# The opening of a hybrid decoder layer: rows normalised tile by tile, small transposes in other banks, the gate product on VectorE, the sample convolution between taps

## The reference, cut to what matters

```python
h = rmsnorm(x, norm_mix_g)
p = einsum('btd,dk->btk', h, w_in)          # 6 blocks of 1024 columns
u_a, v_a, c_val, c_gate, g_a, g_b = split(p)
glu = c_val * sigmoid(c_gate)
padded = concatenate([conv_buf, glu], axis=1)   # prompt: zeros; sample: 30 cached rows
conv = depthwise_conv(padded, conv_w) + conv_b  # 31 taps per channel
y_b = silu(layernorm(conv)) @ w_branch_b + b_branch_b
y_a = (u_a * chunk_spatial_mix(layernorm(gelu(v_a)))) @ w_branch_a
x = x + (sigmoid(g_a) * y_a + sigmoid(g_b) * y_b) @ w_out
x = x + moe(rmsnorm(x, norm_ffn_g))             # top 4 of 32 experts
```

## Time and profile before

| | us |
|---|---|
| median of 3 runs (1359.11 to 1364.49) | 1363.99 |
| the profiled execution, its own time | 1364.04 |
| span of that execution | 1362.3 |
| PE busy | 1196.0 (88%) |
| DVE busy | 584.2 (43%) |
| POOL busy | 494.5 (36%) |
| ACT busy | 255.3 (19%) |
| bytes read from HBM | 447.00 MB, 330 GB/s over the span |

### The profile page before, as it was taken

How to read it: one execution, slowest core, us unless ns; L and a number is a source line. 1 busy time by engine, 2 the same in 40 slices (tenths; PEclk the granted TensorE clock), 3 DMA queues, 4 the chain that set the end, 5 groups by cost and what they waited for, 6 DMA issues and landing times.

```text
span 1362.3 us, 30127 instructions
## 1 busy us (share of the span) xinstructions
PE 1196.0 (88%) x11131; PEld 585.9 (43%) x11132; DVE 584.2 (43%) x1229; ACT 255.3 (19%) x497; POOL 494.5 (36%) x813
## 2 busy tenths in 40 slices
PE   5899999999999997797699779869799798699996
PEld 3677777775543343232233223323234233233333
DVE  0699971211353443433244424424244344244444
ACT  3001122200122221221122112111122121122222
POOL 0183120000141344455444544544445445444330
PEclk9898999999799999998899889989899899899998
DMA  8963333345489599999999999999999999999981
GB/s 255 317 196 108 111 119 124 99 153 220 174 358 382 197 397 418 418 418 417 419 417 416 416 419 418 418 418 418 416 416 417 417 418 414 418 418 409 398 345 59
DMA packets 110953, 448.96 MB, mean 330 GB/s; under 512 B 8526, under 2 KB 42894, under 8 KB 78107
## 3 DMA queue, kind: packets, MB, share of 16 engines
q1 hardware_dynamic: 110190, 446.57, 83.0%
q10 hardware_dynamic: 685, 1.17, 0.3%
q0 software_dynamic: 48, 0.85, 0.2%
HBM read 447.00 MB, written 2.42 MB: 330 GB/s over the span
## 4 chain that ended last, share of the span: by engine, by line
PE 60%; DMA 11%; POOL 8%; issue 8%; DVE 7%; SPq 5%; ACT 0%; DVEq 0%; POOLq 0%
PE banks L1290 21%; PE banks L1093 12%; PE banks L1300 12%; DMA ring<-in_w_down 10%; POOL ring L508 6%; DVE R L762 4%; PE banks L1021 3%; SPq L383 3%; PE banks L1075 3%; PE banks L1054 2%; PE banks L1205 2%; POOL big L477 1%; PE banks L1061 1%; POOL prod L499 1%; PE banks L1084 1%
## 5 line engine op out<-in xcount | busy, mean ns | idle before, releaser
L1290 PE MATMUL banks<-ring,hT 128*32 128x512 f32 x3328 | 441.5, 625 | 99.1 <-POOL ring L508 84.2
L508 POOL COPY ring<-big 128x512 f32<-128x512 f32 x248 | 142.2, 621 | 567.9 <-SPq L389 567.9
L508 POOL COPY ring<-R 128x512 f32<-128x512 f32 x496 | 287.1, 623 | 133.4 <-DMA R<-in_w_up 131.2
L309 DVE TENSOR_TENSOR xt<-xt,banks 128x1024 f32<-128x1024 f32 x106 | 128.8, 1215 | 432.6 <-PE banks L1075 432.6
L1300 PE MATMUL banks<-ring,hT 128*32 128x256 f32 x3328 | 229.8, 396 | 11.5 <-DMA ring<-in_w_down 10.0
L1093 PE MATMUL banks<-hT,ring 128*128 128x288 f32 x768 | 195.6, 417 | 7.9 <-ACT stage L535 6.0
L1290 PEld LDWEIGHTS banks<-ring,hT 128*32 128x32 f32 x3328 | 98.7, 113 | 236.2 <-POOL ring L508 106.5
L1300 PEld LDWEIGHTS banks<-ring,hT 128*32 128x32 f32 x3328 | 110.5, 115 | 196.9 <-issue 129.4
L1093 PEld LDWEIGHTS banks<-hT,ring 128*128 128x128 f32 x768 | 149.3, 196 | 50.6 <-ACT stage L535 6.4
L654 ACT COPY WT<-banks 128x256 f32<-128x256 f32 x52 | 19.4, 372 | 537.9 <-PE banks L1300 537.9
L762 DVE SCALAR_TENSOR_TENSOR R<-big,convw,R 128x256 f32<-128x256 f32 x240 | 99.7, 490 | 0.0
(11 more groups left out here) (225 smaller groups left out, 770.3 us busy)
## 6 DMA issues: line engine op xcount, KB each, us to landing
ring<-in_w_down SPq DMA_DIRECT2D x128, 1024.0 KB, 11.7
R<-in_w_up SPq DMA_DIRECT2D x124, 1024.0 KB, 18.2
ring<-in_w_up SPq DMA_DIRECT2D x70, 1024.0 KB, 9.4
big<-in_w_up SPq DMA_DIRECT2D x62, 1024.0 KB, 14.1
ring<-in_w_in SPq DMA_DIRECT2D x24, 1024.0 KB, 10.0
ring<-in_w_branch_b SPq DMA_DIRECT2D x4, 1024.0 KB, 4.9
ring<-in_w_branch_a SPq DMA_DIRECT2D x4, 1024.0 KB, 4.9
ring<-in_w_out SPq DMA_DIRECT2D x4, 1024.0 KB, 4.9
```

Source lines behind the costliest of these rows:

```text
L309: nc.vector.tensor_tensor(dst, dst, rows, ALU.add).then_inc(y_added, 1)
L508: ins = nc.gpsimd.tensor_copy(ring[:, k, h * 512:(h + 1) * 512], parked[k][:, h * 512:(h + 1) * 512])
L1290: ins = mm(UP[g * BLK:(g + 1) * BLK, :], xT[:, k, :], ring[:, k, g * 512:(g + 1) * 512], start=k == 0, stop=k == UP_SLOTS - 1)
```

## The change

- The eight vector parameters are loaded from ACT's queue instead of SP's.
- ACT loads the root's table first, and squares, roots, scales and turns go tile by tile: DVE scales row tile tt as soon as its own root is there, and PE turns all eight pieces of it. PE runs 16 small matmuls of 128x32 ahead of that. The gain and the other vectors are turned between the second and third row tile. ACT scales the even tiles of `hT` on the way out, DVE the odd ones, and PE starts on each tile as it comes.
- After j = 0 the history is turned into banks 4 to 7 as before, but conv_w goes to bank 2, b_up to bank 3, and the spatial weights to banks 6 and 7; each step of j waits for its own banks.
- The copy of the value (ACT) goes away. DVE multiplies it straight out of PSUM with the sigmoid in `tmpc` (`gate`), tiles 0 and 1 ahead of the convolution, 2 and 3 after pair 0, 4 to 7 between taps of pair 1. PE waits for these products before it uses a bank again, and for all eight only before it turns v.
- DVE's eight sample tiles come between taps of pairs 2 and 3 instead of behind them.

```diff
@@ SP
-            for v, name in enumerate(vec_names):
-                load(vecrows[v * KC:(v + 1) * KC, :], a[name][0].rearrange("(c p) -> c p", p=P), vec_in)
@@ POOL
-            pool.wait_ge(evac_early, 5)
-            for c in range(KC):
-                pool.wait_ge(gate_sig, c + 1)
-                nc.gpsimd.tensor_tensor(cprompt[:, c, HIST:HIST + SEQ], tmpv[:, c % 2, 0:SEQ],
...
             pool.wait_ge(glu_ready, KC)
             nc.gpsimd.tensor_copy(glu_tail[:].rearrange("p c (b t) -> p c b t", b=DB),
                                   csample[:, :, :, HIST:SEG]).then_inc(tail_packed, 1)
 
+            pool.wait_ge(small_copied, 3)
@@ ACT
+            for v, name in enumerate(vec_names):
+                act.dma_start(vecrows[v * KC:(v + 1) * KC, :], a[name][0].rearrange("(c p) -> c p", p=P)
+                              ).then_inc(vec_in, 16)
             act.wait_ge(pads_zero, 1)
+            act.wait_ge(const_ready, 4)
+            load_root_table()
             for tt in range(NT):
...
-            act.wait_ge(const_ready, 4)
-            act.wait_ge(squared, NT)
-            root(ss[:, 4:4 + NT], ss[:, 0:NT], 1.0 / D)
+                act.wait_ge(squared, tt + 1)
+                root(ss[:, 4 + tt:5 + tt], ss[:, tt:tt + 1], 1.0 / D)
 
             act.wait_ge(evac_early, 1)
-            for c in range(KC):
+            for c in range(0, KC, 2):
                 act.wait_ge(x_transposed, c + 1)
...
-                nc.scalar.activation(tmpc[:, c % 2, :], bank[4 * (c // 2 % 2) + 2 + c % 2][:, 0:T], ACT.Sigmoid)
-                nc.scalar.copy(tmpv[:, c % 2, :], bank[4 * (c // 2 % 2) + c % 2][:, 0:T]).then_inc(gate_sig, 1)
+                nc.scalar.activation(tmpc[:, c % 2, :], bank[4 * (c // 2 % 2) + 2 + c % 2][:, 0:T], ACT.Sigmoid
+                                     ).then_inc(gate_sig, 1)
@@ DVE
+            for c in range(1, KC, 2):
+                dve.wait_ge(x_transposed, c + 1)
+                V.tensor_scalar(hT[:, c, :], bank[c][:, 0:T], col(NORM_MIX, c), None, ALU.mult).then_inc(hT_odd, 1)
...
+            def gate(c):
+
+                dve.wait_ge(gate_sig, c + 1)
+                val = bank[4 * (c // 2 % 2) + c % 2]
+                V.tensor_tensor(cprompt[:, c, HIST:HIST + SEQ], val[:, 0:SEQ], tmpc[:, c % 2, 0:SEQ], ALU.mult)
+                V.tensor_tensor(csample[:, c, :, HIST:SEG], val[:, SEQ:T].rearrange("p (b t) -> p b t", b=DB),
+                                tmpc[:, c % 2, SEQ:T].rearrange("p (b t) -> p b t", b=DB), ALU.mult
+                                ).then_inc(glu_ready, 1)
...
+            between = {(0, 30): (gate, (2, 3)), (1, 11): (gate, (4, 5)), (1, 26): (gate, (6, 7)),
+                       (2, 10): (convolve_sample, (0,)), (2, 20): (convolve_sample, (1,)),
+                       (2, 30): (convolve_sample, (2,)), (3, 6): (convolve_sample, (3,)),
+                       (3, 12): (convolve_sample, (4,)), (3, 18): (convolve_sample, (5,)),
+                       (3, 24): (convolve_sample, (6,)), (3, 30): (convolve_sample, (7,))}
@@ PE
+            for _ in range(16):
+                mm(bank[7][:, 320:320 + NE], ones[:], below[:, 0:NE], start=True, stop=True)
...
-            pe.wait_ge(hT_ready, KC)
             for j in range(KC // 2):
+                if j == 1:
+                    pe.wait_ge(history_copied, KC)
                 if j >= 2:
                     pe.wait_ge(gate_sig, 2 * (j - 1))
+                    pe.wait_ge(glu_ready, 2 * (j - 1))
+                if j == 2:
+                    pe.wait_ge(small_copied, 2)
                 for part in range(2):
+                    if j == 1 and part == 1:
+                        pe.wait_ge(small_copied, 3)
...
-            pe.wait_ge(gate_sig, KC)
+            pe.wait_ge(gate_sig, KC - 2)
+            pe.wait_ge(glu_ready, KC - 2)
@@ turn_v
+            if c == 0:
+                pe.wait_ge(gate_sig, KC)
+                pe.wait_ge(glu_ready, KC)
```

More of the change, by code:

```diff
@@ L703, in _ @@
                 r = ROWS[tt]
+                dve.wait_ge(rooted, tt + 1)
+                link(V.reciprocal(ss[:, 4 + tt:5 + tt], ss[:, 4 + tt:5 + tt]))
                 V.tensor_scalar(stage[0:r, tt, :], xs_rows if tt == 2 else xt[:, tt, :], ss[0:r, 4 + tt:5 + tt], None,
                                 ALU.mult).then_inc(xs_ready, 1)
[L707 to L711 removed]
@@ new lines, in _ @@
+            for c in (4, 5, 6, 7, 0, 1, 2, 3):
+                V.tensor_copy(csample[:, c, :, 0:HIST],
+                              bank[4 + c // 2][:, (c % 2) * DB * HIST:(c % 2 + 1) * DB * HIST]
+                              .rearrange("p (b h) -> p b h", b=DB)).then_inc(history_copied, 1)
+            dve.wait_ge(small_turned, 1)
+            V.tensor_copy(convw[:], bank[2][:, 0:KC * W].rearrange("p (c k) -> p c k", c=KC)
+                          ).then_inc(small_copied, 1)
+            dve.wait_ge(small_turned, 2)
@@ L749, in take_x, with convolve @@
                                 ).then_inc(xT_ready, 1)
-            def convolve(pair):
-                for k in range(W):
+            def gate(c):
[5 more added lines that the diff above has]
+                                ).then_inc(glu_ready, 1)
+            def convolve(pair, taps):
+                for k in taps:
                     for c in pair:
@@ L765, in convolve, with convolve_sample @@
                         link.count[0] += 1
-            def convolve_sample(tiles):
-                for c in tiles:
-                    dve.wait_ge(prod_ready, DS * (c + 1))
-                    tail = conv[:, c, SEQ:T]
-                    V.tensor_reduce(tail, prod[:].rearrange("p b t k -> p (b t) k"), AX.X, ALU.add
-                                    ).then_inc(prod_used, 1)
-                    dve.wait_ge(prod_used, c + 1)
-                    V.tensor_scalar(tail, tail, col(CONV_B, c), None, ALU.add).then_inc(conv_done, 1)
+            def convolve_sample(c):
+                dve.wait_ge(prod_ready, DS * (c + 1))
+                tail = conv[:, c, SEQ:T]
+                V.tensor_reduce(tail, prod[:].rearrange("p b t k -> p (b t) k"), AX.X, ALU.add
+                                ).then_inc(prod_used, 1)
+                dve.wait_ge(prod_used, c + 1)
+                V.tensor_scalar(tail, tail, col(CONV_B, c), None, ALU.add).then_inc(conv_done, 1)
+            between = {(0, 30): (gate, (2, 3)), (1, 11): (gate, (4, 5)), (1, 26): (gate, (6, 7)),
[3 more added lines that the diff above has]
+                       (3, 24): (convolve_sample, (6,)), (3, 30): (convolve_sample, (7,))}
             dve.wait_ge(history_zero, 1)
+            gate(0)
+            gate(1)
             for pair in range(KC // 2):
                 dve.wait_ge(glu_ready, 2 * pair + 2)
-                convolve((2 * pair, 2 * pair + 1))
-                if pair == 2:
-                    convolve_sample(range(0, 3))
-            convolve_sample(range(3, KC))
+                for k in range(W):
+                    convolve((2 * pair, 2 * pair + 1), (k,))
+                    if (pair, k) in between:
+                        what, tiles = between[pair, k]
+                        for c in tiles:
+                            what(c)
             dve.wait_ge(v_rows, 2 * KC)
```

79 lines of the change are left out of this document (35 added, 44 removed).

## The result

| us | before | after |
|---|---|---|
| median of six runs each | 1359.61 (1359.11 to 1364.49) | 1349.75 (1346.70 to 1353.98) |
| the profiled execution, its own time | 1364.04 | 1346.70 |
| its span | 1362.3 | 1344.8 |
| start of the mean over channels | 185.25 | 168.76 |
| start of w_out | 317.85 | 303.38 |

The medians differ by 9.9 us. The ratio of the times is 0.9916 (0.99 to 0.9932), which is 11.4 us. Six runs of the kernel before put its median at 1359.6. Four of them lie within 0.6 us of each other, two at about 1364, and the profiled execution, on which the prediction stood, was as long as those two. The profiled execution of after, in turn, is the shortest of its six.

The account below looks back on a forecast made before the run. DVE's stretch was taken to set the start of the mean, with PE nearly level and the end following. 13.6 us won there, less 1.6 for PE's clock, gave 12.0: 1364.04 to 1352.0 us, range 1344 to 1361.

Parts of the forecast that it names:

- The signs: Trace marks named beforehand, such as first projection at 13 to 17 us, first tap at 40 to 45, mean at 170 to 174.
- The base: Starting time of the whole kernel: the profiled execution, 1364.04 us, taken to stand at the median (1363.99).
- Opening: From the start through j = 0: first projection at 14.5 instead of 21.67 us, j = 0 ending at 33.2.
- The loads: SP's queue at the start: w_in and all behind it issued 2.8 us earlier, spatial weights landing at 35.5.
- rival C: Front of the kernel: loads no earlier, transposes slow, taps from 46 to 48 us; net 6 to 8 won, 1357; chance 0.09.
- rival D: Opening: vector parameters land late, taking up to 11.4 of the 12.0 us won, 1363; chance 0.04.
- The samples: DVE's sample tiles between taps of pairs 2 and 3: 3.15 us each, 1.7 of it lost to POOL's batch.
- Rival A: Sample tiles: POOL is held off until DVE stops, costing 8.8 us more, 1361; chance 0.17.
- DVE's stretch: DVE from first tap to last sample tile: 129.4 us, from 42.0 to 171.4, gates and sample tiles included.
- the first burst: POOL's first burst of products beside DVE's taps in pair 2: its loss of 3.4 us left as before.
- PE: PE from j = 1 to the mean: ready at 165.0 us, then over 6 us waiting and about 1.9 in clock.
- Rival B: At the mean: DVE loses nothing or starts earlier, PE sets the mean at 165; 20.1 us won, 1344; chance 0.12.

Follow-up runs that it names:

- e1: The changed kernel with DVE's sample tiles behind pairs 2 and 3 again instead of between taps: 1354.73 us, ratio 0.9948.
- e10: The changed kernel with conv_w and b_up turned into banks 4 and 5 again, and j = 1 after all copies: 1350.55 us, ratio 0.9907.
- e8: The changed kernel with the routing's 12 filling matmuls at 128 columns instead of 32: 1347.01 us, ratio 0.9901.
- e6: The changed kernel with POOL's sample products cut to one column for seven of eight tiles: 1324.34 us, times behind the router not comparable.
- e3: The changed kernel with the gate product as before, ACT copying the value and POOL multiplying: 1350.84 us, ratio 0.9928.
- e7: The changed kernel with e4's copies on ACT, and the sample bias added by ACT after n = 17: 1343.13 us, ratio 0.988.
- e9: The changed kernel with e4, e7 and e8 together: copies and sample bias on ACT, filling matmuls of 128 columns: 1341.36 us, ratio 0.9844.
- e2: The changed kernel with the old opening (parameters on SP's queue, one root, first projection after all tiles): 1355.83 us, ratio 0.9957.
- e11: The kernel before with the routing's 12 filling matmuls at 128 columns: 1358.7 us over ten runs, ratio 0.9974.
- e4: The changed kernel with DVE's copies of history, b_up and spatial weights moved to ACT: 1345.81 us, ratio 0.9887.
- e5: The changed kernel without PE's 16 small matmuls ahead of the row transposes: 1349.8 us, ratio 0.9923.

## Why the prediction was right

Forecast 1352.0, measured 1349.75; a gain of 12.0 us against 9.9 in the medians and 11.4 by the ratio, whose interval (0.99 to 0.9932) is 9.2 to 13.6 us. The mechanism held: DVE is late, PE waits before the mean, and the end follows the mean. The signs came as named (a tap beside POOL took 906 ns in the median of three at 106.5 to 108.2, where I had 885) but for two. The mean started at 168.76, before the 170 to 174 that I had given, and the end moved only roughly with it, by 17.5 us against 16.5.

**The base** was the weakest step. I took the profiled execution to stand at the median, from three runs. Six put the median 4.4 us lower. Taken off that, 12.0 would have given 1347.6, 2.1 us under the measurement. That the forecast lies 2.3 us from the measured time is in part luck: the base was 4.4 us too high, and in the two traces w_out moved by 14.5 us, 2.5 more than I had. The stage behind w_out, which I counted as unchanged, differs between profiles of kernels that are the same there by up to 4.8 us (1041.42 in the changed kernel's, 1046.26 in e1's), and that is 40% of the gain at stake.

**Opening.** Forecast 14.5 for the first projection, measured 16.48: I had taken PE's small matmuls as hidden by the wait for x, and they run 2.4 us beyond it. They took 7.04 us, a price that I had not put on them at all. The term that I left open, the records' rate, gave most of it back: 17.14 us for the step instead of 18.66 (the records were at 406 ns from 21.8 on). Both errors nearly cancel, and j = 0 ends at 33.6 where I had 33.2. That is luck too: with the same opening the step took 15.76 us in e10's profile and 18.45 in e8's.

**The loads** are where one part of rival C held. I had w_in and all behind it issued 2.8 us earlier and w_spatial landing at 35.5; it landed at 38.17. SP's four big loads took 11.66 us to issue instead of 8.44. That did no harm only because DVE, with its copies, had next to no rest from 35.30 on. It was not far from doing some: in e1 and e6 the same weights were turned 1.3 and 1.0 us later, and the first tap came 1.4 and 1.0 later. I had them landed before PE comes to them, but PE waited 0.4 to 0.5 us for them in every profile of the new opening. The parameters, rival D, were in time.

**First tap.** Forecast 42.0, measured 41.49. The two gate products took 0.43 a tile, not 0.6, since they overlap.

**The samples.** The term with the widest bounds (1.45 to 4.1 a tile, taken 3.15) was measured at 3.25 in pair 2 (1.89 for sum and bias, 1.36 in the taps behind) and at some 3.15 in pair 3 (tiles 7.97 apart, less twelve taps of 0.40), and e6 puts the collision itself at 1.83 where I had 1.7. Nearness of situation chose the value well: the batch of before that began as a sum ended was the same thing. Rival A priced full blocking. The rule of the Trainium skill that says the same ("SBUF — State Buffer", section "Who interferes with whom") fits e3's single products of 15.99 and 12.03 us, and not the batches, of which one began between running taps at 92.54 and took 3.27 us for four products. With 12 or 20 taps ahead of it no sum had to wait for its products. What makes the one product stick and the others alternate, the shape, the operands or the moment, was not separated.

**DVE's stretch.** Forecast 129.4 long, ending at 171.4; measured 127.2 to 168.7. The sum of terms was 2.2 too high: the gates by 1.0, the first burst by 0.4 (3.0 instead of 3.4), the rest in small parts.

**PE.** I had it ready at 165.0, it was at 162.1: j = 1 to 3 and n = 0 and 1 ran at the full rate from 39.10 on, without the half clock that the kernel before had there (granted 0.50 from 50.71 to 54.60, within the 48.83 us of the earlier trace rows). The wait before the mean was 6.64 (forecast 6.6), since both ends came earlier than I had them by nearly the same amount (2.9 and 2.8); its price in clock was 2.0 (forecast 1.9). None of the new waits for `glu_ready` was ever seen, and the 5.96 before n = 0 went entirely.

**Rival B**, PE as the bound, was as far away as 6.6 us of waiting say. e6 shows what lies there: with DVE out of the way PE starts the mean at 164.65. In e7 and e9 PE was ready at 164.2 but started at 166.5, for ACT's bias.

| what the change did | us at the mean's start | shown by |
|---|---|---|
| opening tile by tile | 5.9 | e2 |
| samples between taps | 3.9 | e1 |
| gate product on DVE | 2.2 | e3 |
| other banks | 1.4 (up to 2.9) | e10 |
| sum of the four | 13.4 | |
| measured | 16.5 | |

The parts were taken out one at a time, each is read from one profile against one, and such a pair can differ by 1 us without any cause in the program (e8, at 169.74). So they needn't add up; 3.1 us belong to parts taken together or to the run of before (e11's mean, with nothing changed ahead of it, started at 183.34 instead of 185.25).

## What to carry to other kernels

When two engines come to a meeting point nearly together, price a change by the engine that will be late, and look for its work on the other engines: the eleven copies that the change left on DVE (e4, 3.6 us) were worth as much as the eight samples that the change rearranged. A wait that turns into a collision between two engines is not covered for free; the nearest existing collision in the trace priced it well here (1.7 us against 1.83). And compare the stage behind the change in both profiles before reading a difference of spans: here 3 of 17.5 us between the two spans came from the clock in a part of the program that nobody touched.

## What the hardware showed

- Loads of 4 KB taken off the queue in which the big ones stand did not bring these forward: four loads of 1 MB each took 11.66 us to issue instead of 8.44, and the next in line went out within 0.5 us of its old time.
- With filling matmuls of 32 columns PE had its clock granted at 0.50 in the routing, though it was busy nearly all the time (no rest over 0.4 us in the changed kernel), in all nine profiles of kernels that have them and compute everything (before, after, e1 to e5, e7 and e10; for about 7 to 14 us, and the length differs from run to run). With 128 columns it was at 1.00 in all three (e8, e9, e11). That is worth some 3.5 us in e11; in e8 the medians say 2.7, which its interval doesn't resolve.
- The clock at the start of j = 1 differs between runs of almost the same program: 1.00 over 39.1 to 44.1 in the changed kernel, 0.76 in e8 and 0.67 in e7 over 40 to 45, without a difference in PE's busy share that would order them (4.38, 5.10 and 3.98 of the 5.5 us ahead, for the three in this order). It is worth some 2 us to PE at most (48.83 us for the 192 records in the kernel before, against 54.49 for 224 in the changed kernel), and nothing where PE then waits for DVE.
- What the clock costs behind a rest did not grow with the rest: the 16 records of the mean took 7.05 us behind 3.35 us of waiting (e3), 6.17 behind 6.64 (the changed kernel) and 5.53 behind 8.95 (e1). Behind 2.28 (e7), 1.27 (the kernel before) and 0.95 (e11) they took 4.15.
